# Masks of the SSM decay on VectorE, exponentials behind the squares, and a later start of GpSimd's first weight sums

## What is computed

```python
def segsum(a):
    cs = jnp.cumsum(a, axis=-1)
    diff = cs[..., :, None] - cs[..., None, :]
    return jnp.where(mask, diff, -jnp.inf)          # mask: lower triangle, no future rows
...
decay = jnp.exp(segsum(adt))
cb = jnp.einsum("bclhn,bcshn->bhcls", cc, bc)
y_diag = jnp.einsum("bhcls,bcshp->bclhp", cb * decay, xc)
...
y = y * jax.nn.silu(z)                               # gated
yg = yg * lax.rsqrt(jnp.mean(yg * yg, axis=-1, keepdims=True) + NORM_EPS)
...
mixed = jnp.concatenate([attn, ssm], axis=-1) @ w_out[l]
x = x + gate1 * rms_norm(mixed, post_mix_w[l])
```

## Time and profile before

| | before |
|---|---|
| time, median of 3 runs | 1129.91 us (1128.08 to 1131.09) |
| the profiled execution | 1130.47 us, of which its span is 1128.4 us |
| busy: TensorE matmuls | 1079.4 us, 96% of the span |
| VectorE | 870.7 us, 77% |
| ScalarE | 560.4 us, 50% |
| GpSimd | 249.5 us, 22% |
| granted TensorE clock | 0.986 of full speed in the mean |

### The profile page before, as it was taken

How to read it: one execution, slowest core, us unless ns; L and a number is a source line. 1 busy time by engine, 2 the same in 40 slices (tenths; PEclk the granted TensorE clock), 3 DMA queues, 4 the chain that set the end, 5 groups by cost and what they waited for, 6 DMA issues and landing times.

```text
span 1128.4 us, 14880 instructions
## 1 busy us (share of the span) xinstructions
PE 1079.4 (96%) x5096; PEld 868.9 (77%) x5096; DVE 870.7 (77%) x1123; ACT 560.4 (50%) x1012; POOL 249.5 (22%) x235
## 2 busy tenths in 40 slices
PE   4799999999998999889999999999999999999997
PEld 3688766666686888767888888888888888888885
DVE  5869677767559687799889888888888877777687
ACT  4821254545554555565454444445444545554453
POOL 2000011121124442133433333333333100000012
PEclk9699999999999999999999999999999999999999
DMA  9979411001134222225353535343433695622324
GB/s 347 319 242 318 141 38 38 20 20 38 56 115 143 81 94 75 84 85 168 112 167 112 167 112 166 105 164 121 153 109 120 205 390 198 214 95 97 100 85 168
DMA packets 117503, 157.40 MB, mean 139 GB/s; under 512 B 15308, under 2 KB 76237, under 8 KB 117453
## 3 DMA queue, kind: packets, MB, share of 16 engines
q1 hardware_dynamic: 117133, 155.69, 41.1%
q0 software_dynamic: 320, 1.06, 0.3%
HBM read 125.75 MB, written 30.98 MB: 139 GB/s over the span
## 4 chain that ended last, share of the span: by engine, by line
PE 76%; DVE 11%; ACT 4%; DMA 3%; SPq 2%; issue 2%; POOL 1%; DVEq 0%; POOLq 0%; ACTq 0%
PE ps L2459 33%; PE ps L2526 18%; PE ps L2129 18%; DVE big L1408 3%; DMA raw<-in_w_in_dram 2%; PE ps L2168 2%; PE ps L2194 1%; DMA spare<-in_w_ada_dram 1%; PE ps L2182 1%; SPq L490 1%; SPq L481 1%; PE ps L2299 1%; PE ps L2227 1%; POOL st L766 1%; DVE w_lo L1449 1%
## 5 line engine op out<-in xcount | busy, mean ns | idle before, releaser
L2129 PE MATMUL ps<-a_hi,w_hi 128*128 128x512 f32 x416 | 141.8, 419 | 6.6 <-DVE a_lo L1468 3.2
L2129 PE MATMUL ps<-a_lo,w_hi 128*128 128x512 f32 x416 | 132.3, 396 | 0.0
L2129 PE MATMUL ps<-a_hi,w_lo 128*128 128x512 f32 x416 | 131.4, 394 | 0.0
L2526 PE MATMUL ps<-w_hi,a_hi 128*128 128x512 f32 x308 | 119.9, 389 | 0.2 <-DVE a_lo L1961 0.2
L2526 PE MATMUL ps<-w_lo,a_hi 128*128 128x512 f32 x308 | 119.8, 389 | 0.0
L2526 PE MATMUL ps<-w_hi,a_lo 128*128 128x512 f32 x308 | 119.8, 389 | 0.0
L1320 ACT ACTIVATE w_hi<-raw 128x512 fp32r<-128x512 f32 x77 | 48.7, 632 | 98.4 <-PE ps L2526 88.0
L2129 PEld LDWEIGHTS ps<-a_hi,w_hi 128*128 128x128 f32 x416 | 72.9, 191 | 28.3 <-issue 15.3
L1237 ACT ACTIVATE scratch<-ps 128x512 f32<-128x512 f32 x88 | 52.1, 593 | 85.4 <-PE ps L2459 85.4
L2129 PEld LDWEIGHTS ps<-a_hi,w_lo 128*128 128x128 f32 x416 | 79.0, 190 | 18.1
L2129 PEld LDWEIGHTS ps<-a_lo,w_hi 128*128 128x128 f32 x416 | 79.2, 190 | 17.7
(11 more groups left out here) (271 smaller groups left out, 2399.5 us busy)
## 6 DMA issues: line engine op xcount, KB each, us to landing
big<-in_w_ada_dram SPq DMA_DIRECT2D x20, 1024.0 KB, 8.9
raw<-in_w_up_dram SPq DMA_DIRECT2D x23, 512.0 KB, 5.1
big<-in_w_down_dram SPq DMA_DIRECT2D x22, 512.0 KB, 6.5
down_weight_sums<-big SPq DMA_DIRECT2D x22, 512.0 KB, 3.4
raw<-down_weight_sums SPq DMA_DIRECT2D x44, 256.0 KB, 2.8
ffn_hidden<-big SPq DMA_DIRECT2D x21, 512.0 KB, 2.6
big<-ffn_hidden SPq DMA_DIRECT2D x21, 512.0 KB, 8.2
big<-in_w_up_dram SPq DMA_DIRECT2D x20, 512.0 KB, 4.7
```

What stands on the lines that cost most here:

```text
L2129: mm = pe.matmul(out, lhs_of[a], rhs_of(b, j), start=first and p == 0, stop=last and p == 2)
L2526: mm = pe.matmul(bk, a[:, ts], rhs_op(s)[w], start=fresh and m == 0, stop=last and m == 2, skip_group_check=s // KH in (J6, J3, J7))
```

## The change

The masks of chunks 3 to 7 leave GpSimd's list and go to VectorE's, between `mixed_lo_attention` (with what follows it in chunks 4 and 6) and `ssm_rows`. On ScalarE the squares of the gated rows and the exponentials change places. GpSimd's first weight sums get a wait for chunk 3's finished SSM rows.

```diff
@@ GpSimd, turn i
                     pool.wait_ge(s_q2, b + 1)
                     rstd(st[:, 40 + b:41 + b], st[:, 32 + b:33 + b], D, s_r2)
-                if 2 <= i < NB - 1:
-                    decay_mask(i + 1)
                 if i < NB:
                     pool.wait_ge(s_gq, i + 1)
                     rstd(st[:, 58:60], st[:, 56:58], SSM_W // GROUPS, s_gr)
@@
                 if i == 3:
+                    pool.wait_ge(s_my, 4)
                     weight_sums(0, 0, first=True)
@@ ScalarE, turn i
                     x1_squares(i - 2)
                     mixed_hi_attention(i)
+                    gated_squares(i)
                     if i + 1 < NB:
                         for g in range(GROUPS):
                             decay_exp(i + 1, g)
-                    gated_squares(i)
                     x1_evacuate(i - 2)
@@ VectorE, turn i
                     elif i == 7:
                         token_sum("t3", EARLY)
+                    if i < NB - 1:
+                        decay_mask(i + 1)
                     ssm_rows(i)
```

## The result

| | before | after |
|---|---|---|
| median of 9 runs each | 1130.41 us (1128.02 to 1131.09) | 1135.14 us (1132.78 to 1139.42) |
| ratio, 95% interval | | 1.0051 (1.0039 to 1.0063) |
| the profiled execution, its span | 1130.47 us, 1128.4 us | 1139.42 us, 1137.6 us |
| granted TensorE clock in the mean | 0.986 | 0.976 |

The change makes the kernel slower by half a per cent, 4.7 us between the medians; 1134.9 us was forecast.

The account below looks back on a forecast made before the run. TensorE, busy nearly throughout, was taken as the bound, so other engines matter only through its waits. Chunk losses 0.64 + 0.48 + 1.67 + 0.63 + 1.62 = 5.0 us on 1129.91 gave 1134.9 us, range 1130.5 to 1137.5.

Parts of the forecast that it names:

- Part 1: Masks from GpSimd to VectorE: 1.29 us for the pair, exponentials 0.72 us behind the first mask, L1794's gain unused.
- Part 2: ScalarE's exponentials behind the squares: in chunk 5, L1085 1.37 us late and L1073 0.53 late, delaying TensorE's projection.
- 0.64, 0.48 and 0.63: Forecast losses in us for chunks 3, 4 and 6; the one for chunk 4 includes the sums' new wait.
- L1810 chain: L1073, GpSimd's two tiny steps, L1694, L1810, then TensorE's projection; 0.53 us late by this path for chunk 6.
- bank path: TensorE's transposes wait until L1085 has left their bank; the projection is 0.63 us late by this path for chunk 6.
- the larger counts: 0.63: Chunk 6's projection: of two late paths, 0.63 us by the bank and 0.53 by L1810, the larger was taken.
- 1.67: Loss in us at chunk 5's projection: exponentials and L1085 2.51 late behind a token operand, less L1073's 0.84.
- Part 3: GpSimd's first weight sums wait: TensorE's 0.7 us wait gained and lost again, L764 0.73 late, net +0.48 in chunk 4.
- What would show it: Trace signs, among them TensorE waits in chunks 3 to 7, some 0.5 us in three and 1.6 in chunks 5 and 7.
- hidden: Rival: ScalarE's late L1085 finds more room than 0.68 us; 1131.2 us, no change that can be told; chance 0.16.
- dearer: Rival: VectorE's masks run at L1787's price beside GpSimd, 4.4 us more; 1139.3 us; chance 0.08.
- faster: Rival: GpSimd's masks made the chunks slow; without them TensorE's 3.6 us of waits go; 1126.3 us; chance 0.06.

Follow-up runs that it names:

- e6: Masks on VectorE in its idle time ahead of L1789, ScalarE's order and the sums as in the kernel before; ratio 1.0002 against before.
- e4: The changed kernel with the masks ahead of the token operands in chunks 4 and 6; ratio 1.0017 against before.
- e1: The kernel before with ScalarE's swap alone, gated squares ahead of the exponentials; ratio 0.9996 against before.
- e5: The changed kernel without the wait of GpSimd's first weight sums; ratio 1.0036 against before.
- e8: The changed kernel run once more, for a second profile; ratio 1.0040 against before.
- e7: The changed kernel with x1 taken out of PSUM ahead of the exponentials on ScalarE; ratio 1.0089 against before.
- e2: The kernel before with the masks alone moved to VectorE, ScalarE's order and the sums as before; ratio 1.0164 against before.
- e3: The kernel before with only the wait of GpSimd's first weight sums for chunk 3's SSM rows; ratio 1.0008 against before.
- e10: GpSimd's first weight sums one turn later, on top of the kernel with VectorE's masks ahead of L1789; ratio 0.9995 against before.
- e9: The kernel before with GpSimd's first weight sums one turn later, in chunk 4; ratio 1.0003 against before.

## Why the prediction was right, and where its steps were off

- **The range and the direction**: forecast 1134.9, measured 1135.14. The likeliest case is the one that came. That the two lie 0.2 us apart is in part luck: the forecast starts from a median of 1129.91 us, which nine runs put at 1130.41, its sum is 0.6 us larger than the chunks at full clock give, and it had nothing for the clock.
- **Part 1, masks.** Right: 1.28 us for the pair, exponentials 0.72 us behind the first mask, L1794 with no idle time, nobody waiting for these rows. L1787, 1.57 us beside GpSimd's mask in the earlier trace rows, takes 0.68 now, and the time of the kernel doesn't gain by it. The rule on shared SBUF interfaces in the Trainium skill, GPSIMD Engine Reference, section 8 (Key points), agrees with these two durations. e6, which has that relief too and no late exponentials, is at 1.0002.
- **Part 2, the late queue.** Right in its mechanism: e4 and e6 move the first mask and the loss follows it, e1 has the swap without the loss. The terms in the three chunks without a token operand in front were 0.64, 0.48 and 0.63 and measured 0.49, 0.36 and 0.51 (the first profile), all of them 0.12 to 0.15 too large. The next two points say why.
- **Which path decides.** TensorE's projection can wait for the bank path or for the L1810 chain, and a constant distance tells which. These are the starts of L1810 and of the projection behind it, chunks 5 and 6, before and after (the earlier trace rows has the projections of before, at 417.31 and 435.06):

```profile
416.53 0.68 DVE L1810 TENSOR_TENSOR w_lo<-ps,w_hi 128x512 fp32r<-128x512 f32 x1
...
434.28 0.68 DVE L1810 TENSOR_TENSOR w_lo<-ps,w_hi 128x512 fp32r<-128x512 f32 x1
```

```profile
422.80 0.68 DVE L1809 TENSOR_TENSOR w_lo<-ps,w_hi 128x512 fp32r<-128x512 f32 x1
...
423.58 0.70 PE L2130 MATMUL ps<-a_hi,w_hi 128*128 128x512 f32 x2
...
441.08 0.68 DVE L1809 TENSOR_TENSOR w_lo<-ps,w_hi 128x512 fp32r<-128x512 f32 x1
...
441.86 0.70 PE L2130 MATMUL ps<-a_hi,w_hi 128*128 128x512 f32 x2
```

  All four distances are 0.78 us, where the rows show a wait for L1810 (0.37 us at 417.31) and where they show none. Chunk 3 has it too (0.79 before, 0.78 after), and chunk 4 after (0.78); chunk 4 before has 1.02, behind TensorE's wait for L1623. So the projection follows the L1810 chain in both kernels, and the bank's wait of 0.55 us ahead of chunk 6's transposes doesn't set its start. The time between those transposes and the projection shrank from 4.23 to 4.05 us.
  - In chunks 3 and 6 the step "the larger counts: 0.63" was wrong. The path that it set aside had 0.53. L1072 stands 7.95 us behind L1788 in chunk 6, and 7.44 before, so it came 0.51 late, and that is what the chunk lost. The bank path was too dear since its room in front of the projection was taken as 0.12 us, the gap behind L2306's end in the rows; by the 4.23 and 4.05 us it was at least 0.18.
  - In chunk 5 the step had the right path, and 1.67 was mis-sized by 0.25. L1072 came 1.64 us late as forecast, but GpSimd's first tiny step (L764) at the head of the chain took 0.44 us before, beside VectorE's token operand, and 0.19 now that it comes when VectorE is idle, and 1.42 was measured. The bank path's 1.52 is nearer, but that path doesn't decide.
  - In chunk 7 the chain decides in plain sight, in e5's profile by a wait of 0.56 us on top of the bank's 1.91, and 1.61 was measured for 1.62.
- **Part 3, the sums.** Right: chunk 3's rows take 0.88 us, L764 behind the sums has no idle time. The projection starts 12.39 us behind L1788, and 11.92 before, so it is 0.47 late for the 0.48 forecast. The chunk lost only 0.36, because 0.11 us came back between the projection's start and the next L1788 (6.25 us, 6.36 before), where the forecast let nothing come back. e5 gives +0.01 for the +0.07 that the text had without the wait.
- **The sum**: 5.0 forecast, 4.4 from the chunks at full clock. The medians differ by 4.7 and the ratio says 5.8 (4.4 to 7.1), in e8's runs of the same kernel 4.5 (2.8 to 6.3). What the sum did not have is TensorE's clock.
- **What would show it**: "TensorE waits for L1810 or for L1085's bank" held in all five chunks, though the bank's waits, 5.3 us in sum, are not the measure of the loss. The rivals hidden, dearer and faster are excluded by the waits, by the 1.28 us of the pair, and by e6.

## What to carry to other kernels

Moving work to a faster engine was free here at a place where that engine waits; the same instructions cost nothing ahead of such a wait (e6) and 2 to 5 us behind it (e4, the change). What to look at is the consumer's queue: find the last idle time in front of it, here 0.68 us on ScalarE, and compare it with how late the new input comes. Which of two late paths decides is told by a distance that stays the same in both kernels (0.78 us from L1810 to the projection), and not by the largest wait on show. When a queue is late as a whole, another order of it only changes which wait shows it (e7).

## What the runs showed of the hardware that was not expected

TensorE's granted clock fell to its lower level (0.50 of full, 1.2 against 2.4 GHz) for a few microseconds behind some of TensorE's waits, in some executions and not in others. The windows of the changed kernel's first profile behind the waits at 361 and 457 us (stretch, length, busy time of TensorE, its weight loads, VectorE, ScalarE and GpSimd, clock, DMA share, GB/s):

```profile
360.00:364.00 4.00, 2.63 (x17) 2.66 (x17) 4.00 (x6) 0.38 (x1) 0.73 (x2) 0.79 0.00 0
364.00:368.00 4.00, 4.00 (x11) 3.16 (x11) 3.32 (x6) 1.67 (x3) 1.06 (x2) 0.50 0.55 217
...
456.00:460.00 4.00, 2.81 (x13) 2.55 (x13) 1.72 (x2) 2.54 (x7) 0.73 (x2) 0.73 0.00 0
460.00:464.00 4.00, 4.00 (x17) 3.71 (x17) 3.86 (x6) 1.67 (x3) 0.64 (x2) 0.50 0.30 121
```

The first stretch follows a wait of 1.56 us that the kernel before has too, at full clock; it made chunk 2 of this execution 3.3 us longer. All twelve profiles have that wait, and the clock falls behind it in four of the six with late masks (the change, e2, e7, e8) and in none of the six without, although the edits don't act before 367 us; why is not shown. The second follows the new wait of 1.91 us and cost 4.13 - 1.61 = 2.5 us in chunk 7, in e8 1.0 us, in e5 nothing. It is no privilege of the change: e1, e3, e6 and e10, where the wait in chunk 7 is 1.0 us as before, show the same fall and 1.6 to 1.7 us, while the profiles of before and of e9 do not. So the fall hangs on more than the length of the wait just ahead of it. These are single profiles. Whether the change makes such falls more frequent, which would explain that the first ratio is rather above 4.4 us than at it, stays open: nine runs of it reach from 1132.78 to 1139.42 us, the shortest two with a mean clock of 0.986 and 0.979, the longest two with 0.976 and 0.977.
